# Six direct units ahead of 19 pair products, with the order of VectorE's work around them rewritten

## The reference

```python
h2 = rmsnorm(x, norm2_g[l])
ffn = (jax.nn.silu(h2 @ w_ffn_gate[l]) * (h2 @ w_ffn_up[l])) @ w_ffn_down[l]
x = x + ffn
```

## Time and profile before

| | us |
|---|---|
| median of 3 runs | 2520.96 (2519.36 to 2524.88) |
| the profiled execution, its own time | 2519.33 |
| its span, first to last instruction | 2517.6 |
| TensorE busy | 2447.0 (97%) |
| VectorE busy | 1231.4 (49%) |
| ScalarE busy | 794.6 (32%) |
| GpSimd busy | 641.4 (25%) |

### The profile page before, as it was taken

The page is one execution under the profiler, slowest core; times in us unless marked ns, Lnnn a source line. Parts: engine busy times, 40 slices in busy tenths (PEclk is TensorE's granted clock), DMA queues, the critical chain, the costliest instruction groups (busy, mean ns, idle before and its releaser), DMA issues.

```text
span 2517.6 us, 29872 instructions
## 1 busy us (share of the span) xinstructions
PE 2447.0 (97%) x11312; PEld 2002.7 (80%) x11312; DVE 1231.4 (49%) x1617; ACT 794.6 (32%) x1157; POOL 641.4 (25%) x332
## 2 busy tenths in 40 slices
PE   8999999989999989999999999999999999999997
PEld 6887888868888878888888888877877877878886
DVE  4424573654444443345321111477777777753534
ACT  4411122232333231134311111254554554541221
POOL 2221122254554432122221121212111112112221
PEclk9998899999999999999999999999999999999998
DMA  3110122232222242212222224233323323344223
GB/s 127 42 42 30 62 76 100 75 127 91 76 82 83 88 143 91 92 59 76 93 100 84 78 95 136 89 104 109 117 77 98 106 77 108 109 150 142 91 94 109
DMA packets 66149, 234.65 MB, mean 93 GB/s; under 512 B 7936, under 2 KB 8080, under 8 KB 66064
## 3 DMA queue, kind: packets, MB, share of 16 engines
q1 hardware_dynamic: 51376, 179.98, 21.8%
q10 hardware_dynamic: 14688, 53.48, 5.2%
HBM read 175.76 MB, written 57.67 MB: 93 GB/s over the span
## 4 chain that ended last, share of the span: by engine, by line
PE 95%; DVE 3%; issue 1%; DMA 0%; ACT 0%; DVEq 0%; SPq 0%; POOL 0%; ACTq 0%
PE dense L676 22%; PE dense L678 22%; PE dense L677 22%; PE dense L830 5%; PE dense L831 5%; PE dense L832 5%; PE aux L955 2%; PE aux L939 2%; PE aux L940 1%; PE aux L968 1%; PE aux L967 1%; PE aux L784 1%; PE aux L781 1%; PE aux L902 1%; DVE residual L1715 1%
## 5 line engine op out<-in xcount | busy, mean ns | idle before, releaser
L676 PE MATMUL dense<-x_hi,w_hi 128*128 128x512 f32 x2000 | 812.2, 406 | 12.8 <-DVE x_lo L1474 11.7
L678 PE MATMUL dense<-x_hi,w_lo 128*128 128x512 f32 x2000 | 785.9, 393 | 0.0
L677 PE MATMUL dense<-x_lo,w_hi 128*128 128x512 f32 x2000 | 785.6, 393 | 0.0
L577 POOL TENSOR_TENSOR w_lo<-w_raw,w_hi 128x1024 fp32r<-128x1024 f32 x157 | 381.3, 2429 | 1445.5 <-ACT w_hi L1027 1438.1
L1027 ACT CAST w_hi<-w_raw 128x1024 fp32r<-128x1024 f32 x156 | 163.8, 1050 | 938.8 <-PE dense L678 915.7
L676 PEld LDWEIGHTS dense<-x_hi,w_hi 128*128 128x128 f32 x2000 | 380.0, 190 | 84.7 <-issue 15.2
L678 PEld LDWEIGHTS dense<-x_hi,w_lo 128*128 128x128 f32 x2000 | 378.6, 189 | 82.0
L677 PEld LDWEIGHTS dense<-x_lo,w_hi 128*128 128x128 f32 x2000 | 380.4, 190 | 68.3 <-issue 1.2
L1515 DVE TENSOR_TENSOR work<-dense,rstd 128x1024 f32<-128x1024 f32 x95 | 116.0, 1221 | 418.1 <-PE dense L678 410.5
L612 POOL TENSOR_TENSOR w_lo<-w_sums,w_hi 128x512 fp32r<-128x512 f32 x80 | 121.0, 1523 | 141.8 <-ACT w_hi L1167 141.8
L676 PE MATMUL dense<-work_split,w_hi 128*128 128x512 f32 x352 | 139.0, 395 | 1.1 <-DVE work L1767 1.1
(11 more groups left out here) (236 smaller groups left out, 3337.1 us busy)
## 6 DMA issues: line engine op xcount, KB each, us to landing
w_raw<-weights SPq DMA_DIRECT2D x177, 512.0 KB, 3.7
kept_qkv<-work ACTq DMA_DIRECT2D x24, 512.0 KB, 2.7
kept_m<-work ACTq DMA_DIRECT2D x22, 512.0 KB, 2.6
work<-kept_m SPq DMA_DIRECT2D x22, 512.0 KB, 3.5
w_raw_b<-weights SPq DMA_DIRECT2D x20, 512.0 KB, 4.4
residual<-xT SPq DMA_DIRECT2D x16, 512.0 KB, 6.7
kept_x<-residual ACTq DMA_DIRECT2D x16, 512.0 KB, 2.6
att_q<-kept_qkv SPq DMA_DIRECT2D x32, 256.0 KB, 4.0
```

The source lines that it names most:

```text
L577: pool.tensor_tensor(WL[:, u.slot], WR[:, u.slot], WH[:, u.slot].bitcast(f32), ALU.subtract).then_inc(w_lo, 1)
L676: pe.matmul(dst, WH[:, u.slot, k], hi, start=(k == 0), stop=False)
L677: pe.matmul(dst, WH[:, u.slot, k], lo, start=False, stop=False)
L678: last = pe.matmul(dst, WL[:, u.slot, k], hi, start=False, stop=(k == nk - 1))
```

## The change

- Six direct units (33 to 38) and 19 pairs, instead of four and 20. Pair p now makes tile 3 + p.
- The accumulators change banks: B7 and B5 move to slot 1, B1 and B6 to slot 0. The last direct unit is in slot 0 both before and after. So products 0 and 1 of the first pair wait for the evacuation of the last but one direct unit, and product 2 for that of the last.
- The residue of sum 2 moves from GpSimd to VectorE.
- VectorE's list: evacuations stand ahead of the sums that they were queued behind; `weight_sums(0)` comes after the fifth evacuation; the fourth `lo_again` comes behind the first pair's joins.
- In the last pair, VectorE's joins come ahead of `m_lo(2)` and `m_lo(3)`, and `m_lo(5)` behind the last product of gate and up; SyncE loads m tiles 2 and 3 ahead of the two weight units 77 and 78.
- Which half of `w_hi` a product takes is shifted by one at pairs 4, 8 and 12, so that the last pair ends on the same halves as before. At each shift a half is written again after three products instead of four.
- The first pair's weights go to `w_raw` and wait for the last direct unit's weight residue, instead of to `w_raw_b` early.
- The matmuls that spread the norm's `rstd` stand behind group 12 of unit 33 instead of group 15 (a group is 3 matmuls).

```diff
-U_GU, TILES, DIRECT, DUOS = 33, 22, 4, 20
+U_GU, TILES, DIRECT, DUOS = 33, 22, 6, 19
+T_DUO = DIRECT // 2
...
-        B7, B5, B1, B6 = 0, 1, 2, 3
+        B7, B5, B1, B6 = 2, 3, 0, 1
...
-            return (7 * p + i + 2) % 4
+            return (7 * p + i + 2 + min(p // 4, 3)) % 4
...
         def w_pair(p):
-            return WR if p % 2 else WRB
+            return WRB if p % 2 else WR
...
-            load_m(0)
-            load_m(1)
+            for t in range(4):
+                load_m(t)
             sp.wait_ge(w_sum, 4 * DUOS)
             sp.wait_ge(d_lo, 6 * DUOS)
...
-                                g15=[lambda: spread(2, WK[:, TMP + 3])]))
+                                g12=[lambda: spread(2, WK[:, TMP + 3])]))
...
             for p in range(DUOS):
-                pe.wait_ge(evac, U_DUO)
                 if p:
                     pe.wait_ge(joined, 4 * p)
                 else:
+                    pe.wait_ge(evac, U_DUO - 1)
                     pe.wait_ge(t_lo, 1)
                 times(p, 0, TX[:, 0, 0], TX[:, 0, 1], B7, True)
...
                 if p:
                     pe.wait_ge(p12, p)
                 else:
+                    pe.wait_ge(evac, U_DUO)
                     pe.wait_ge(b_lo, 1)
                 times(p, 2, XHV[:, 0, :, left], XLV[:, 0, :, left], B1, True)
```

ScalarE's list at the first pair, in the code:

```diff
                 hi_half(p, 4)
-                store_m(p + 1)
+                if p == 0:
+                    hi_again(0, 1)
+                store_m(T_DUO + p - 1)
                 hi_half(p, 5)
                 keep_p1(p)
+                if p == 0:
+                    hi_again(1, 1)
                 hi_half(p, 6)
-                if p == 0:
-                    hi_again(0, 1)
-                    hi_again(1, 1)
                 hi_half(p + 1, 0)
```

More of the change, by code:

```diff
@@ L321, in two_blocks @@
         sp_x2, sp_m, m_in = sem("sp_x2"), [sem("sp_m0"), sem("sp_m1")], [sem("m_in0"), sem("m_in1")]
-        xn, t_sum, t_hi, t_lo, t_lo_pool = (sem(n) for n in ("xn", "t_sum", "t_hi", "t_lo", "t_lo_pool"))
+        xn, t_sum, t_hi, t_lo = (sem(n) for n in ("xn", "t_sum", "t_hi", "t_lo"))
         b_hi, b_lo = sem("b_hi"), sem("b_lo")
@@ L348, in half, with held @@
         def half(p, i):
-            return (7 * p + i + 2) % 4
+            return (7 * p + i + 2 + min(p // 4, 3)) % 4
+        def held(p, i):
+            same = [r for r in range(7 * p + i) if half(r // 7, r % 7) == half(p, i)]
+            return (same[-1] // 7, same[-1] % 7) if same else None
         def w_pair(p):
-            return WR if p % 2 else WRB
+            return WRB if p % 2 else WR
         def quarter(p, i):
@@ L462, in _ @@
                              ).then_inc(w_raw[u.slot], 16)
-            for t in range(2, 8):
+            for t in range(4, 8):
                 load_m(t)
@@ L840, in _ @@
                 else:
+                    pe.wait_ge(evac, U_DUO - 1)
                     pe.wait_ge(t_lo, 1)
                 times(p, 0, TX[:, 0, 0], TX[:, 0, 1], B7, True)
-                pe.wait_ge(evac, U_DUO + 2 * p)
-                if p == 0:
+                if p:
+                    pe.wait_ge(evac, U_DUO + 2 * p)
+                else:
                     pe.wait_ge(t_lo, 2)
@@ L1156, in hi_half @@
             def hi_half(p, i):
-                q = 7 * p + i
-                if q < 4:
-                    act.wait_ge(mm_done, U_DUO - 1 + q // 2)
+                if held(p, i) is None:
+                    act.wait_ge(mm_done, U_DUO - 1 + i // 2)
                 else:
-                    act.wait_ge(*product((q - 4) // 7, (q - 4) % 7, prod, mm_done))
+                    act.wait_ge(*product(*held(p, i), prod, mm_done))
                 if i in (0, 1, 3, 6):
@@ L1204, in _ @@
             hi_sum(1, XV[:, 0, :, HALF:S])
+            split(Unit(U_GU + 4))
+            silu_gate(1)
+            hi_sum(2, XSUM[:])
+            split(Unit(U_GU + 5))
+            store_m(1)
             hi_half(0, 0)
             hi_half(0, 1)
-            silu_gate(1)
-            hi_sum(2, XSUM[:])
+            silu_gate(2)
             hi_half(0, 2)
@@ L1731, in _ @@
             lo_sum(1, b12)
+            dve.wait_ge(sp_m[0], 16)
+            scaled(Unit(U_GU + 3), m_buffer(1))
+            gated_tile(1)
             dve.wait_ge(t_lo, 2)
@@ L1734, in _ @@
             dve.tensor_tensor(b12, b21, XSUM[:], ALU.subtract).then_inc(t_sum, 1)
-            dve.wait_ge(sp_m[0], 16)
-            scaled(Unit(U_GU + 3), m_buffer(1))
+            lo_sum(2, XSUM[:])
+            dve.wait_ge(m_t, 2)
+            scaled(Unit(U_GU + 4), GATE)
+            weight_sums(0)
+            dve.wait_ge(sp_m[1], 16)
+            scaled(Unit(U_GU + 5), m_buffer(2))
+            gated_tile(2)
             lo_again(0, 0, 0)
-            gated_tile(1)
             lo_again(1, 1, 0)
             lo_again(2, 0, 1)
-            lo_again(3, 1, 1)
             for p in range(DUOS):
-                up = m_buffer(p + 2)
+                t = T_DUO + p
+                up = m_buffer(t)
                 if p == DUOS - 1:
-                    for t in range(4):
-                        m_lo(t)
+                    m_lo(0)
+                    m_lo(1)
                 dve.wait_ge(prod, 6 * p + 4)
@@ L1757, in _ @@
                 dve.tensor_tensor(up[:, right], up[:, right], bank(B5), ALU.add).then_inc(joined, 1)
+                if p == 0:
+                    lo_again(3, 1, 1)
                 if p < DUOS - 1:
@@ L1760, in _ @@
                 else:
-                    m_lo(4)
+                    m_lo(2)
+                    m_lo(3)
                 dve.wait_ge(prod, 6 * p + 6)
@@ L1769, in _ @@
                 dve.wait_ge(p12, p + 1)
-                dve.wait_ge(s_t, p + 3)
+                dve.wait_ge(s_t, t + 1)
                 dve.tensor_tensor(up, GATE, up, ALU.mult).then_inc(m_t, 1)
+            m_lo(5)
             m_lo(6)
```

26 lines of the change are left out of this document (9 added, 17 removed).

## The result

The changed kernel took 2501.39 us, the median of four runs (2497.41 to 2504.6), against 2522.92 us for the kernel before (four runs, 2519.36 to 2525.75). The ratio is 0.9917, 95% interval 0.9900 to 0.9934: 0.8% faster; the medians lie 21.5 us apart. The prediction was 2503, between 2498 and 2510.

A forecast was written before the change was run, and what follows sets the result against it. TensorE, busy 97% of the span, was taken as the bound, so only matmuls and its idle time count. 2519.33 + 2.5 - 12.2 - 7.0 = 2502.6, put at 2503 us for the median; range 2498 to 2510 (8 in 10).

The forecast's parts named there:

- Matmuls, +2.5: Two direct units replace one pair: 96 matmuls for 84, adding 2.5 us.
- Entry, -12.2: From direct units into the first pairs: 3.3 us lost instead of 15.5, a gain of 12.2.
- The meeting before product 2: First pair: GpSimd gets the shared ports before VectorE's recast residue, costing 1.3 us; bounds 0 and 1.3.
- the waits named as a sign of being right: About 1 us before product 2, under 2 before pair 1's product 0, about 2 before unit 77.
- Pair 1's product 0: Start of pair 1: weight sums behind the fourth residue delay the join product 0 needs; 1.8 us lost.
- the fourth residue's 0.2: First pair: the fourth recast residue, behind the joins, ends after product 6 is due; 0.2 us lost.
- less waiting: Rival, chance 0.17: VectorE gets the ports first or ScalarE is later; entry loses 0 to 1, exit 1.2; 2499 us.
- the likeliest case: The forecast itself, chance 0.55: 2501 to 2505.5 us, with 3.3 us lost at entry and 2.2 at exit.
- Steady pairs, 0: Shifted w_hi halves at pairs 4, 8 and 12 cost 0; the cover is at least 3 us.
- Exit, -7.0: Last pair up to unit 77: joins no longer wait for tile loads; 2.2 us lost instead of 9.2, gaining 7.0.
- no longer stand ahead: Entry: weight sums, 3.7 us, leave their place before unit 35's evacuation, so VectorE's following work ends earlier.
- no fall behind 3.37 us: TensorE's clock did not fall after 3.37 us idle; three close short waits might still lower it, giving 2505.

The follow-up runs named there:

- half_first: Changed kernel with ScalarE's cast of product 3's weights ahead of the first x_hi recast; unit 32's evacuation to unit 77 took 440.0 us, against 439.3.
- shift_each: Changed kernel with the w_hi half shifted at each of pairs 1 to 15, not only 4, 8 and 12; unit 32's evacuation to unit 77: 439.2 us.
- exit_only: Kernel before with only the last pair's new join order and m loads; unit 32's evacuation to unit 77: 450.5 us against 457.9, ratio 0.9968.
- sum_first: Changed kernel with VectorE's last sum and its residue back ahead of unit 36's evacuation; unit 32's evacuation to unit 77: 439.3 us, as unaltered.
- four_direct: Changed kernel with four direct units and 20 pairs, the rest adapted; unit 32's evacuation to unit 77: 442.4 us; ratio to the kernel before 0.9945.
- banks_only: Kernel before with only the accumulators' banks exchanged and TensorE's waits adapted; unit 32's evacuation to unit 77: 457.8 us against 457.9, ratio 1.0000.
- four_recast: four_direct with the first x_lo recast residue ahead of sum 2's residue; unit 32's evacuation to unit 77: 444.6 us against 442.4.

## Why the prediction was right, and where its terms were off

*Matmuls, +2.5.* Measured: TensorE has 12 more matmuls (11324 for 11312), units 10.88 us apart and pairs 19.32: +2.4.

*Entry, -12.2.* The long wait and its slow clock are gone, as are the waits before products 2 and 5. Unit 38 ends at 527.3, 18 pairs later it would be 875.1, and the last pair starts at 876.7 (L1782 at 877.01): 1.6 lost instead of 15.5, a gain of 13.9, where I had 3.3 lost. Three terms were too large. The meeting before product 2: I gave GpSimd the ports and 1.3 us; the trace shows VectorE asking at 530.47 and GpSimd at 530.49.

```profile
530.49 3.41 POOL L618 TENSOR_TENSOR w_lo<-w_sums,w_hi 128x512 fp32r<-128x512 f32 x1 [1.02 <-ACT w_hi L1170]
```

GpSimd then took 3.41 us for 1.3 of work and product 2 started in time: 0 lost. So the first of the waits named as a sign of being right, about 1 us before product 2, did not come; it was the lower of the two bounds. Pair 1's product 0 waited 1.2 for L1778, where I had 1.8, and the fourth residue's 0.2 did not appear. These two do not hang on the meeting's 1.3 us: in half_first, which loses 0.9 before product 2, pair 1 still waits 1.1 and product 6 not at all. So the rival "less waiting" was right about the product 2 half of the entry, and the likeliest case about pair 1 and the exit.

*Steady pairs, 0.* Right; shift_each has 15 pairs with the shorter slack, and none is longer.

*Exit, -7.0.* Last pair's product 0 at 876.7, unit 77 due at 896.0, started at 897.92: 1.9 lost instead of 9.2, so -7.3. I had 2.2. The chain was as written, with L1767's successor held up by tile 4's residue (895.83, 1.23 long, so until 897.06). exit_only, which has this part alone, gives -7.4.

*What I gave as causes.* I put the entry's gain down to the list's new order and to the units without saying how much each brings. The runs do: order, banks and the residue's place together 8.1, two units 3.1 net. With six units the banks are worth 0.6, the place of sum 2's residue and the spread nothing. That the weight sums "no longer stand ahead" was a step of the prediction; whether it was needed no run shows, since sum_first moved another piece.

*The total.* The interval gives -18.6; ratios of whole executions allow -17 to -25. The profiled execution's own -15.8 holds 2.65 us of a later unit 32 that is no part of the change. That the forecast of 2503 lies 1.6 us from the measured median is partly luck, as four executions of the kernel spread over 7 us and I had the gain 1.9 us too small; the interval is the better test of it.

## What to carry to other kernels

When one stage hands over to another, add up the helper engine's whole list between them before moving single steps: two cheap cures (a better order, more work of the old kind as cover) may treat the same lateness, and the second then adds only a part. Name the successor of each wait with its own due time; here two of the four forecast appeared, within 0.6 us of their size (pair 1 and unit 77), and the two others (1.3 and 0.2 us) did not. And where executions of one kernel scatter by more than the effect, compare between two marks inside the trace that enclose the change.

## What the hardware showed that was not expected

- A wait of about 3.4 us before a product went either way. The granted clock stayed at 1.00 behind 3.37 in before and exit_only and 3.43 in four_direct; it fell behind 3.37 in banks_only (0.83 in 530 to 540) and behind 3.34 in four_recast (0.72 in 509 to 515), at a cost of 1.6 and 1.5 us. Waits of 5.6 to 9.7 us were followed by a lower clock each time. So the prediction's "no fall behind 3.37 us" was the reading of one trace and not a safe one.
- The scatter of this kernel's runs (2515.9 to 2527.7 for before in one series) comes largely from ahead of the change: unit 32's evacuation starts between 453.8 and 462.0 in the fourteen traces, while what follows unit 77's first matmul lasts 1600.1 to 1605.2. In 190 to 250 and in 250 to 320, with TensorE busy all the time, the granted clock is 0.82 to 0.88. The two traces in which it is 0.83 in both stretches (four_direct, half_first) are those with the latest unit 32 (462.0 and 461.9). Why the clock is lower there was not looked into.
- A meeting on the ports that changes TensorE's schedule by 1 us was decided by 0.02 to 0.04 us, and went the same way in all eight traces of this arrangement: GpSimd's row starts that much behind VectorE's, and the three recast residues take 8.88 or 8.89 us in each.
